# Joining the two heads' score products in a two-layer attention encoder on one Trainium2 core

## What is computed

```python
for l in range(2):                        # 256 + 512 tokens, model width 1024
    h = rms_norm(x, attn_norm)
    q_g, k_g, v_g, q_d, k_d, v_d = split(h @ w_in)
    # grouped attention: 8 query heads, 2 key/value heads, head width 64
    s = einsum('bqkgd,bskd->bkgqs', q, k) * scale
    o_g = einsum('bkgqs,bskd->bqkgd', softmax(s), v)
    # differential attention: 4 heads, two maps each
    p = softmax(q1 k1) - lam * softmax(q2 k2);  o_d = rms_norm(p @ v_d) * (1 - lambda_init)
    x = x + concat(o_g, o_d) @ w_out
    x = x + (silu(gate) * up) @ w_down    # gate, up from rms_norm(x) @ w_gate_up
y = rms_norm(x, final_norm)
```

## Time and profile before

| | |
|---|---|
| median of 3 runs | 1961.39 us (1960.48 to 1961.62) |
| the profiled execution | 1963.19 us |
| its span in the trace | 1961.0 us |
| mean granted TensorE clock | 0.982 of full speed |
| busy: PE / PEld / DVE / ACT / POOL | 93% / 81% / 60% / 42% / 11% |

### The profile page before, as it was taken

How to read it: one execution, slowest core, us unless ns; L and a number is a source line. 1 busy time by engine, 2 the same in 40 slices (tenths; PEclk the granted TensorE clock), 3 DMA queues, 4 the chain that set the end, 5 groups by cost and what they waited for, 6 DMA issues and landing times.

```text
span 1961.0 us, 30279 instructions
## 1 busy us (share of the span) xinstructions
PE 1820.1 (93%) x11280; PEld 1588.2 (81%) x11280; DVE 1183.5 (60%) x2035; ACT 824.1 (42%) x1811; POOL 214.3 (11%) x311
## 2 busy tenths in 40 slices
PE   5999997797999999999999999878969999999998
PEld 5887765686898989899888877656769999999896
DVE  4656777546675656556555467774556566656564
ACT  3234777524342424242333357773343433333242
POOL 2301123204000000000012012231320000000000
PEclk9999999998999999999999999999999999999999
DMA  4221000020222213221221200002112212122222
GB/s 150 64 65 43 1 1 1 26 82 10 77 76 65 76 54 92 59 87 44 65 65 54 65 23 0 1 0 64 44 34 84 88 44 86 48 82 65 65 65 86
DMA packets 121884, 107.86 MB, mean 55 GB/s; under 512 B 3472, under 2 KB 95760, under 8 KB 121776
## 3 DMA queue, kind: packets, MB, share of 16 engines
q1 hardware_dynamic: 120096, 100.74, 17.3%
q0 software_dynamic: 960, 3.28, 0.5%
q10 hardware_dynamic: 720, 2.36, 0.3%
HBM read 103.22 MB, written 3.15 MB: 54 GB/s over the span
## 4 chain that ended last, share of the span: by engine, by line
PE 80%; DVE 7%; ACT 6%; issue 4%; POOL 2%; DMA 1%; ACTq 0%; DVEq 0%; SPq 0%; POOLq 0%
PE bank L1624 14%; PE bank L1626 13%; PE bank L1625 13%; PE bank L1933 11%; PE bank L1937 11%; PE bank L1935 11%; PE bank L1709 4%; ACT stage L884 2%; PE bank L1700 2%; PE bank L1862 1%; DMA x<-in_x_prompt_dram 1%; POOL hrstd L574 1%; DVE stage L1327 1%; PE bank L1695 1%; DVE stage L1320 1%
## 5 line engine op out<-in xcount | busy, mean ns | idle before, releaser
L1624 PE MATMUL bank<-w_hi,hT_hi 128*128 128x512 f32 (+1 forms) x624 | 240.4, 385 | 3.7 <-DVE hT_lo L1339 3.1
L1626 PE MATMUL bank<-w_hi,hT_lo 128*128 128x512 f32 (+1 forms) x624 | 234.5, 376 | 0.0
L1625 PE MATMUL bank<-w_lo,hT_hi 128*128 128x512 f32 (+1 forms) x624 | 234.1, 375 | 0.0
L1709 PEld LDWEIGHTS bank<-v,stage 128*128 128x128 f16 x2400 | 111.6, 102 | 53.7 <-issue 44.9
L1197 DVE TENSOR_TENSOR x<-x,bank 128x512 f32<-128x512 f32 x120 | 81.4, 687 | 119.3 <-PE bank L1626 118.7
L1709 PE MATMUL bank<-v,stage 128*128 (+1 forms) x2400 | 128.6, 208 | 23.2 <-DVE stage L1327 13.2
L1624 PEld LDWEIGHTS bank<-w_hi,hT_hi 128*128 128x128 f32 x624 | 118.7, 190 | 24.8 <-DVE hT_lo L1339 3.8
L1626 PEld LDWEIGHTS bank<-w_hi,hT_lo 128*128 128x128 f32 x624 | 118.4, 190 | 21.6
L572 POOL TENSOR_TENSOR ms<-ss,eps_col 128x1 f32<-128x1 f32 x30 | 9.3, 311 | 1147.8 <-ACT headsq L738 1147.8
L1076 DVE TENSOR_TENSOR w_lo<-w_raw,w_hi 128x1024 fp32r<-128x1024 f32 x44 | 53.8, 1223 | 133.9 <-ACT w_hi L691 133.9
L1625 PEld LDWEIGHTS bank<-w_lo,hT_hi 128*128 128x128 f32 x624 | 118.8, 190 | 19.0
(11 more groups left out here) (209 smaller groups left out, 4673.9 us busy)
## 6 DMA issues: line engine op xcount, KB each, us to landing
x_raw<-in_w_gate_up_dram SPq DMA_DIRECT2D x44, 512.0 KB, 5.1
w_raw<-in_w_gate_up_dram SPq DMA_DIRECT2D x44, 512.0 KB, 4.0
w_raw<-in_w_in_dram SPq DMA_DIRECT2D x36, 512.0 KB, 3.6
w_raw<-in_w_down_dram SPq DMA_DIRECT2D x36, 512.0 KB, 3.8
w_raw<-in_w_out_dram SPq DMA_DIRECT2D x16, 512.0 KB, 3.7
x_raw<-in_w_down_dram SPq DMA_DIRECT2D x8, 512.0 KB, 4.4
out_dram<-stage SPq DMA_DIRECT2D x6, 512.0 KB, 2.6
gain<-in_gains_dram POOLq DMA_DIRECT2D x5, 512.0 KB, 4.7
```

Of the source, the lines that this page charges most:

```text
L1624: pe.matmul(out, a_hi, b_hi, start=first, stop=False)
L1625: pe.matmul(out, a_hi, b_lo, start=False, stop=False)
L1626: return pe.matmul(out, a_lo, b_hi, start=False, stop=last)
L1709: last = pe.matmul(out, probT[:, b, a, k, :], v[i][:, k0 // P + k, at(vcol, width)], start=(k, a, i) == terms[0], stop=(k, a, i) == terms[-1])
```

## The change

The two heads' scores of a tile are issued by one call, product by product in turn (head 0's first product, head 1's first, head 0's second, and so on), with one wait for the exponential of head 1 of the tile two before. In the grouped pairs the call stands behind the second head's transposes, where head 0's scores stood behind the first head's; at tile 5 head 1's scores move ahead of P(5,0). On VectorE max(t+2,0) for t = 2 to 4 moves from ahead of take(t-1) to behind low(t,1).

```diff
@@ VectorE, gqa_pair
                     probT_low(l, e0 + t, t, 0, 0, P_SCALE)
                     inverse_sums(l, e0 + t, t)
-                    if t >= 2 and t < T - 1:
-                        row_max(l, e0 + (t + 2), (t + 2) % T, 0)
                     if t:
                         take_product(l, e0 + (t - 1), t - 1)
                     probT_low(l, e0 + t, t, 1, 1, P_SCALE)
+                    if t >= 2 and t < T - 1:
+                        row_max(l, e0 + (t + 2), (t + 2) % T, 0)
@@ TensorE
-            def scores(l, e, t, h, split=None, first=False):
+            def scores(l, e, t, split=None, first=False):
...
                 if not first:
-                    pe.wait_ge(exp_done.sem, exp_done.at(l, (e - 2) * 2 + h))
-                rows = slice(h * HD, (h + 1) * HD)
-                mm3(bank[:, 2 * b + h, 0:S], q_hi[rows, t * P:(t + 1) * P], q_lo[rows, t * P:(t + 1) * P],
-                    k_hi[rows, k0:k0 + S], k_lo[rows, k0:k0 + S], True, True).then_inc(scores_done.sem, 1)
+                    pe.wait_ge(exp_done.sem, exp_done.at(l, (e - 2) * 2 + 1))
+                cols = slice(t * P, (t + 1) * P)
+                for i, (q, k) in enumerate(((q_hi, k_hi), (q_hi, k_lo), (q_lo, k_hi))):
+                    for h in range(2):
+                        rows = slice(h * HD, (h + 1) * HD)
+                        last = pe.matmul(bank[:, 2 * b + h, 0:S], q[rows, cols], k[rows, k0:k0 + S], start=i == 0,
+                                         stop=i == 2)
+                        if i == 2:
+                            last.then_inc(scores_done.sem, 1)
@@ TensorE, gqa_pair
                         if t == 0 and h:
-                            scores(l, e + 3, 3, 0)
-                            scores(l, e + 3, 3, 1)
-                        if t >= 2:
-                            scores(l, e + 2, (t + 2) % T, h, p * 2 + 2 if t == 4 and h == 0 else None)
+                            scores(l, e + 3, 3)
+                        if t >= 2 and h:
+                            scores(l, e + 2, (t + 2) % T, p * 2 + 2 if t == 4 else None)
...
                 gqa_transpose(l, e, t, 1)
-                scores(l, e0 + (T + 1), 1, 0)
+                scores(l, e0 + (T + 1), 1)
                 gqa_product(l, p, t, 0, vcol)
-                scores(l, e0 + (T + 1), 1, 1)
                 gqa_product(l, p, t, 1, vcol)
-                scores(l, e0 + (T + 2), 2, 0, p * 2 + 3)
-                scores(l, e0 + (T + 2), 2, 1)
+                scores(l, e0 + (T + 2), 2, p * 2 + 3)
```

More of the change, by code:

```diff
@@ L1783, in diff_pair @@
                     if t and (t + 2 < T or following):
-                        for h in range(2):
-                            scores(l, e0 + (t + 2), (t + 2) % T, h, p * 2 + 2 if t == 4 and h == 0 else None)
+                        scores(l, e0 + (t + 2), (t + 2) % T, p * 2 + 2 if t == 4 else None)
                     diff_transpose(l, p, t)
@@ L1870, in _ @@
                         pe.wait_ge(v_rest.sem, v_rest.at(l, T + 2 * t + 1))
-                    for h in range(2):
-                        scores(l, t, t, h, {(0, 0): 0, (2, 0): 1}.get((t, h)), first=t < 2)
+                    scores(l, t, t, {0: 0, 2: 1}.get(t), first=t < 2)
                 with pe.Fori(0, 2) as kv:
```

## The result

The changed kernel takes 1974.8 us (median of 4 runs, 1972.6 to 1978.3) against 1961.5 before: ratio 1.0070, 95% interval 1.0052 to 1.0087, 13.3 us slower. Timed again beside the kernel before on another occasion it was 1973.6 against 1960.8, ratio 1.0067 (1.0054 to 1.0081). The forecast was 1968.3, 6.9 us slower, and the range 1961 to 1976 holds the result. The profiled execution took 1974.6 us with a span of 1972.4.

The account below looks back on a forecast made before the run. The prediction took the attention stage to look TensorE-bound, with ScalarE held by the moved maximum after the change. Eight grouped pairs 0.86 us longer add 6.9 us to the median 1961.4, giving 1968.3 us, range 1961 to 1976.

Parts of the forecast that it names:

- What bounds the stage: Attention stage: looks bound by TensorE, busy 20.5 of 22.0 us per grouped pair, VectorE and ScalarE 16 each.
- The P(t,0) wait for low: Grouped pair, tiles 3 to 5: TensorE stands idle 0.7 to 1.5 us ahead of P(t,0), released by low.
- The joined scores: Both heads' six products take about 0.90 us, the second head free; issuing in turn costs nothing.
- Rivals 4 and 5: Joined places: issuing in turn pays, 1965.4 us, chance 0.04; or it undoes the overlap, 1975.5 us, chance 0.02.
- The walk: Hand-over times followed through one grouped pair: TensorE's freed 2.9 us become idle time, the pair gets 0.86 us longer.
- The held exponential: Tiles 2 to 4: exp(t+2,0) waits on ScalarE for the moved max(t+2,0), idle more than 1 us.
- the 0.86: Walked lengthening of each grouped pair in us, M to M 22.9 in place of 22.0.
- The sum: Eight grouped pairs, 0.86 us longer each: 6.9 us, giving 1968.3 us.
- the clock's term: Rival: new idle time lowers TensorE's clock once a grouped pair, 7 us more, 1975.3 us; chance 0.09.
- Rivals 1 and 2: Grouped pairs: exp(t+2,0) isn't held, 23 us go, 1938, chance 0.12; or gain and loss balance, 1961.4, chance 0.15.

Follow-up runs that it names:

- joined_by_head: The changed kernel with the six score products issued head by head, three of head 0 then three of head 1: 1974.4 us against 1962.1 before the change.
- joined_max_old: The changed kernel with max(t+2,0) back ahead of take(t-1) and low(t,1), scores still joined: 1951.3 us, ratio 0.9940 to the kernel before.
- filling: The changed kernel with unread identity transposes where TensorE waits for low(t,0), at tiles 0, 1, 3, 4, 5: 1966.9 us; changed kernel beside it 1973.6.
- exp_shifted: The changed kernel with exponentials of tiles 4, 5, 0' and 1' one place back and their maxima refitted: 1953.1 us against 1960.8 before the change.
- joined_max_old_again: Second timing of joined_max_old, the changed kernel with the maximum back in its old place: 1950.8 us against 1960.0 before the change.

## Why the prediction was right in its way and short in its size

**What bounds the stage.** Right: with the scores joined TensorE no longer sets the end of a pair. The P(t,0) wait for low, as named.

**The joined scores.** Right: 0.90 us for six products, and in turn or head by head are the same; the earlier trace rows had shown it. By that, the Trainium skill's rule (page "TensorE: Matmul & The Clock Gate", "Part 3: Packing small matmuls — row/col tiling", that matmuls start in program order) isn't what this case shows: in the kernel before and in joined_by_head head 1's first product starts in the same tenth of a microsecond as head 0's (216.9 and 239.6), with two products of head 0 between them in the stream. Rivals 4 and 5 fall by joined_by_head, whose S(2') to M is 0.90 us in the other order too. (The walk's 2.9 us freed per pair are not seen as such: TensorE's busy time in a pair at full clock falls by 1.8 to 1.9, from 20.52 to 18.70 in joined_max_old and 18.61 in the changed kernel; the longer P(2,0) below is part of the rest.)

**The held exponential.** Right, and right in size: M to M 22.88 us at full clock in the first layer, walked 22.86 (in the second it is 1.0 longer than before, where 0.86 was walked). joined_max_old against the changed kernel shows that the moved maximum brings it; the 0.86 is the balance of some 1.0 us gained by the joined scores and 1.9 lost by the maximum. The waits ahead of P(4,0) and P(5,0) were as walked, the one ahead of P(3,0) was 0.33 us, under the 0.7 named. One detail was off without effect: P(2,0) to M takes 1224.31 - 1223.15 = 1.16 us in place of 0.59, but the mix copy waits for exp(4,0) there in any case.

**The sum.** This is where it fell short; the range still held the result. I took the clock's term as nothing ("The new idle times are some 1.5 us, so I hold it unlikely", 0.09) and made it a rival to the walk, when it adds to it. Eight pairs at full clock are 4 x 0.88 + 4 x 0.97 = 7.4 us longer, so that of the 12.7 and 13.3 us measured 5.3 to 5.9 are left for the clock; filling brought 6.6 us back, nearly all of them by the clock. The step that failed is the inference from one idle time: the earlier trace rows showed the clock fall after 2.5 us in which TensorE did nothing, and I took idle times of up to 1.5 as safe. The trace of the kernel before already spoke against that, in the first layer's differential pairs:

```profile
368.11 1.28 PE L1709 MATMUL bank<-v,stage 128*128 128x128 bf16 x20 [1.25 <-DVE hT_lo L1339]
370.86 1.12 PE L1700 MATMUL bank<-ident,stage 128*128 128x128 f32 x4 [1.48 <-DVE stage L1320]
```

```profile
367.50:370.50 3.00, 1.28 (x20) 1.13 (x20) 2.45 (x5) 3.00 (x7) 1.07 (x3) 0.99 0.00 0
370.50:373.90 3.40, 3.04 (x25) 2.97 (x25) 2.85 (x4) 1.36 (x4) 0.72 (x1) 0.50 0.60 159
```

When the clock went to 0.50 at 370.5, the last idle time had been of 1.25 us and one of 1.48 was still running (busy 1.28 of 3.00 us). The changed kernel did the same after 1.40 us, with shorter ones near it (busy 1.60 of 3.00 us), but not in every pair. The rival's own price, 7 us more, was near, but in part by luck. It was one fall in every grouped pair, and in the first profile that is nearly what happened, in four of the six pairs from M to M. In the second it happened in one of six, and most of the added time at the lower clock lies in the differential pairs (about 12 us more of it than before, against about 4 in the grouped part; I work this estimate out from the lengths and clocks of the table).

**Rivals 1 and 2** (TensorE is what counts; gain and loss balance) fall: no pair of the changed kernel is as short as 22.0. Rival 1's gain of 23 us isn't had by joined_max_old or exp_shifted either: joining the scores takes 1.8 us of TensorE's busy time out of a pair and shortens it by 1.0, and in joined_max_old exponentials still wait for maxima (0.73, 0.16, 0.41 us).

**Not settled.** Why the second layer's pairs at full clock are 0.3 us shorter than the first's (21.7 against 22.0 before the change) wasn't looked into. The spread between executions goes with the granted clock: of 26 executions of the kernel before timed beside joined_max_old_again the shortest, 1954.4 us, had a mean clock of 0.985 and the longest, 1970.2, had 0.976. Why one execution loses more clock than the next isn't known, nor why filling helps behind the pairs that it fills.

## What to carry to other kernels

When work of the busiest engine is joined and moved later, look at each in-order stream that consumes it: an instruction that has to wait for the later result should stand where its engine would have been idle anyway, and must not be put behind another hand-over of the engine that waits for it. Walk one period with hand-over times read from the trace before moving anything; here that gave the period to 0.02 us in one layer and 0.1 in the other. Then ask what the idle time on TensorE does to its clock, and add that to the walk: it added 5 to 6 us to some 7 here, and filling the idle time with work nobody reads gave 6.6 back.

## What the runs showed that was not expected

- The clock falls in pairs in which TensorE is busy for 19.3 to 20.1 of 24.0 us, in one place after pieces of idle time none over 1.40 us; in other pairs with the same idle times it doesn't. Adding 24 transposes to a pair of 22.9 us made the kernel 6.6 us faster.
- The same twenty small products with v take 0.59 us from the first to the next instruction in one place and 1.16 to 1.38 in another. Their weight loads are spread likewise, over 1.15 us, without waits for another engine between them:

```profile
1223.15 1.15 PEld L1714 LDWEIGHTS bank<-v,stage 128*128 128x128 f16 x20 [0.37 <-issue]
```

  against, in the kernel before,

```profile
226.26 0.64 PEld L1709 LDWEIGHTS bank<-v,stage 128*128 128x128 f16 x20 [0.37 <-issue]
```

  In both kernels the stream of these products has register arithmetic between them, since v's column depends on the loop. Whether that is what takes the time wasn't tried.
